# The down product of a feed-forward stage by seven block products, with y collected in the output

## What is computed

```
hm = rmsnorm(x, g_mlp_norm)
y  = x + square(relu(hm @ w_up)) @ w_down      # w_up 2048 x 8192, w_down 8192 x 2048, float32
```

## Time and profile before

| what | value |
|---|---|
| median of 3 runs | 2805.25 us (2804.82 to 2809.1) |
| profiled execution, its own time | 2809.45 us |
| its span, first to last instruction | 2808.0 us |
| mean granted TensorE clock | 0.996 of full speed |
| PE busy, share of the span | 99% |
| DVE / ACT / POOL busy | 56% / 34% / 8% |
| feed-forward stage | from 1412.9 us to the end |

### The profile page before, as it was taken

The page is one execution under the profiler, slowest core; times in us unless marked ns, Lnnn a source line. Parts: engine busy times, 40 slices in busy tenths (PEclk is TensorE's granted clock), DMA queues, the critical chain, the costliest instruction groups (busy, mean ns, idle before and its releaser), DMA issues.

```text
span 2808.0 us, 57688 instructions
## 1 busy us (share of the span) xinstructions
PE 2790.3 (99%) x22723; PEld 2745.9 (98%) x22723; DVE 1578.6 (56%) x2763; ACT 960.5 (34%) x1484; POOL 224.3 (8%) x341
## 2 busy tenths in 40 slices
PE   8999999999999999999999999999999999999999
PEld 8999999999999999999999999999999999999999
DVE  6433544454444454445576556665556665566658
ACT  5435433333333342222243223332233332333322
POOL 2100122210000010013300000000000000000000
PEclk9999999999999999999999999999999999999999
DMA  6533233322222224444433333332333323333235
GB/s 199 185 100 106 81 111 97 109 95 92 96 87 94 88 90 151 136 126 137 135 110 99 97 97 113 104 104 90 101 115 105 99 81 103 97 105 97 91 96 186
DMA packets 89562, 309.39 MB, mean 110 GB/s; under 512 B 11714, under 2 KB 12098, under 8 KB 89360
## 3 DMA queue, kind: packets, MB, share of 16 engines
q1 hardware_dynamic: 70112, 247.49, 27.8%
q0 software_dynamic: 16208, 55.42, 6.1%
q10 hardware_dynamic: 3168, 5.45, 0.6%
HBM read 287.23 MB, written 27.37 MB: 112 GB/s over the span
## 4 chain that ended last, share of the span: by engine, by line
PE 75%; issue 18%; DVE 3%; POOL 2%; ACT 1%; DMA 1%; POOLq 0%; SPq 0%; ACTq 0%; DVEq 0%
PE mm L540 25%; PE aux L919 13%; PE mm L919 13%; PE mm L863 12%; PE aux L863 9%; PE mm L614 1%; PE aux L645 1%; POOL z L2090 1%; DVE w_lo L1769 1%; ACT w_hi L1197 0%; PE aux L761 0%; POOL merge_d L2091 0%; DVE w_lo L1287 0%; PE aux L554 0%; PE aux L659 0%
## 5 line engine op out<-in xcount | busy, mean ns | idle before, releaser
L1287 DVE TENSOR_TENSOR w_lo<-w_raw,w_hi 128x512 fp32r<-128x512 f32 x392 | 283.3, 724 | 630.5 <-ACT w_hi L968 629.5
L1769 DVE TENSOR_TENSOR w_lo<-w_raw,w_hi 128x1024 fp32r<-128x1024 f32 x288 | 352.9, 1225 | 390.8 <-ACT w_hi L1197 158.1
L540 PE MATMUL mm<-a_hi,w_hi 128*128 128x260 f32 x2624 | 550.1, 291 | 3.2 <-DVE rel_s L1322 1.6
L540 PE MATMUL mm<-a_hi,w_lo 128*128 128x260 f32 x2624 | 532.1, 285 | 0.0
L540 PE MATMUL mm<-a_lo,w_hi 128*128 128x260 f32 x2624 | 532.1, 285 | 0.0
L1197 ACT ACTIVATE w_hi<-w_raw 128x1024 fp32r<-128x1024 f32 x288 | 297.5, 1057 | 661.0 <-PE mm L919 431.2
L968 ACT ACTIVATE w_hi<-w_raw 128x512 fp32r<-128x512 f32 x392 | 246.4, 629 | 692.8 <-PE mm L540 672.6
L540 PEld LDWEIGHTS mm<-a_hi,w_hi 128*128 128x128 f32 x2624 | 409.0, 191 | 10.2 <-DVE w_lo L1287 3.0
L540 PEld LDWEIGHTS mm<-a_lo,w_hi 128*128 128x128 f32 x2624 | 409.5, 191 | 0.0
L540 PEld LDWEIGHTS mm<-a_hi,w_lo 128*128 128x128 f32 x2624 | 408.3, 190 | 0.0
L863 PE MATMUL mm<-at_t,w_hi 128*128 128x260 f32 x2048 | 373.3, 284 | 1.1 <-DVE w_lo L1769 1.1
(11 more groups left out here) (320 smaller groups left out, 4161.4 us busy)
## 6 DMA issues: line engine op xcount, KB each, us to landing
w_raw<-in_w_ff SPq DMA_DIRECT2D x256, 512.0 KB, 3.6
w_raw<-in_w SPq DMA_DIRECT2D x200, 512.0 KB, 3.6
merge_d<-z POOLq DMA_DIRECT2D x32, 260.0 KB, 2.4
g_in<-merge_d POOLq DMA_DIRECT2D x16, 520.0 KB, 4.9
x_back<-x_d POOLq DMA_DIRECT2D x8, 520.0 KB, 9.1
pages<-in_cache_cmp POOLq DMA_DIRECT2D x16, 256.0 KB, 3.3
w_cmp<-in_w_cmp POOLq DMA_DIRECT2D x8, 512.0 KB, 4.8
stage<-in_cache_sel POOLq DMA_DIRECT2D x32, 128.0 KB, 2.5
```

Of the source, the lines that this page charges most:

```text
L540: last = pe.matmul(mm[:, 2 * v + h, 0:HT], w, a[:, kt, h * HT:(h + 1) * HT], start=first and k == 0 and part == 0, stop=final and k == CK ...
L1287: dve.tensor_tensor(w_lo[:, c, :], raw(u, c), w_hi[:, c, :].bitcast(F32), ALU.subtract).then_inc(lo_split, 1)
L1769: dve.tensor_tensor(ring_lo(i), fold(source(i)), ring_hi(i).bitcast(F32), ALU.subtract).then_inc(ff_lo, 1)
```

## The change

- The down part also goes by seven block products. A group's 16 y tiles are taken in four pieces (D0 to D3) of four y tiles; a piece is two row pairs (m = 0, 1), and each has seven products of 2 contraction steps times 3 matmuls. The contraction of 512 rows is one block row pair of 2 x 256.
- The hidden tiles become the token side of that product. They need the same seven combinations (B11 ... T2): three sums per r, made by POOL (`hidden_sums`), and their hi and lo (`hidden_hi`, `hidden_lo`) over all seven, in the arrays `fb_mid` and `fb_end`. The norm's factor is now multiplied in at the hidden rows (`hidden`, with `r_ff`), and ACT takes the square.
- Each piece needs weight sums: one (a21 + a22) by POOL (`weight_sum`), two by DVE (`down_sum`). The same sum of the up pairs moves from DVE to POOL. A piece has four hi and lo entries, three of 128x1024 and one of 128x512.
- The results of a piece are copied from PSUM by ACT (`copies`, `copy_c21`), combined by DVE (`cs_in`) in `y_mid`, and added to `y_t` in DRAM by two DMAs of 520 KB with `accum_op` on POOL's queue (`tiles_added`). `y_acc` and the ending `y_out` are gone; x2, the residual, is stored to `y_t` itself.
- The order is turned: the down pieces of group g-1 stand between the up parts of group g: U0, D0, D1, U1, D2, D3. Group 0 has U0 and U1 alone, and a last round has D0 to D3 alone. lo too has a ring of three buffers.

The core of the diff:

```diff
+            def up_part(p):                                   # PE
+                for b in range(2):
+                    pe.wait_ge(ff_lo, p.e + b + 1)
...
+                    product(p, b)
+                up_rest(p)
...
+            def down_product(p, b, m, js=(0, 1)):
+                hi, lo = ring_hi(p.slot(D_ENTRY[b])), ring_lo(p.slot(D_ENTRY[b]))
+                dst = bank((2 if b == 1 else 4 if b in (3, 5) else p.x) + m)
+                fb = fb_of(p.g - 1)
+                for j in js:
+                    o = m * 2 * P + j * P
+                    wh, wl = (w[:, D_SIDE[b], o:o + P] for w in (hi, lo))
+                    o = TIMES[b] * HT
+                    for w, e, part in ((wh, o, 0), (wh, A_HALF + o, 1), (wl, o, 2)):
+                        last = pe.matmul(dst, w, fb[:, j, e:e + HT],
...
-            def down_part(g, u, kts, hs=(0, 1)):
...
-                    for w, a, part in ((wh, fb_hi, 0), (wh, fb_lo, 1), (wl, fb_hi, 2)):
-                        for h in hs:
-                            last = pe.matmul(bank(o + h), w, a[:, kt, h * HT:(h + 1) * HT],
...
+            def freed_by_down(p, k):                          # SP
+                sp_.wait_ge(ff_lo, p.e + 3 + k)
+                return p.slots[k]
...
+            def up_part(p):                                   # DVE
...
+                    ff_lo_in(p, 1)
+                    up_sum(p, 1)
...
+                    if conv:
+                        hidden_lo(p.g - 1, 0, 0)
+                    ff_lo_in(p, 2)
+                ff_lo_in(p, 3)
+                if conv:
+                    hidden_lo(p.g - 1, 0, 1)
+                up_sum(p, 2)
+                ff_lo_in(p, 4)
...
+            def down_part(p):
...
+                    ff_lo_in(p, 1)
+                    down_sum(p, 1)
+                ff_lo_in(p, 2)
+                if not late:
+                    cs_in(p, 0)
+                ff_lo_in(p, 3)
...
+                if to and to.up:
+                    ff_lo_in(to, 0)
+                    up_sum(to, 0)
+                if whole(p.g, NG - 1) and p.n == D3:
+                    for n in range(2):
+                        hidden_lo(NG - 1, 0, n)
+                cs_in(p, 1)
+                cs_in(p, 2)
...
+            def weight_sum(p):                                # POOL
+                if p.up:
+                    a21, a22 = (w_raw[:, n, :] for n in p.slots[2:])
+                    pool.wait_ge(ff_sum, p.sums + 1)
+                    pool.wait_ge(ff_loaded[p.slots[3]], p.loads())
+                else:
+                    a21, a22 = (w_raw[:, p.slots[0], k * CW:(k + 1) * CW] for k in range(2))
+                    pool.wait_ge(ff_loaded[p.slots[0]], p.loads())
+                pool.tensor_tensor(a21, a21, a22, ALU.add).then_inc(ff_s1, 1)
+
+            def hidden_sums(g, r):
...
+                pool.tensor_tensor(ts[:, 0:2, :], c[:, 1:4:2, :], c[:, 0:2, :], ALU.subtract).then_inc(t_made, 1)
+                pool.wait_ge(t_made, n + 1)
+                pool.tensor_tensor(ts[:, 2, :], c[:, 3, :], ts[:, 0, :], ALU.subtract).then_inc(t_made, 1)
+                pool.wait_ge(t_made, n + 2)
+                pool.tensor_tensor(c[:, 1, :], c[:, 2, :], ts[:, 2, :], ALU.subtract).then_inc(t_made, 1)
+
+            def tiles_added(p):
+                y, first = y_buffer(p)
+                pool.wait_ge(ff_read, p.read + 3)
+                pool.wait_ge(ff_c21, p.c21 + 2)
...
+                for m in range(2):
+                    k = 4 * p.q + 2 * m
+                    pool.dma_start(t["y_t"][k:k + 2].rearrange("m p (h c) -> p m h c", h=2), y[:, m, :, :, :],
+                                   accum_op=ALU.add).then_inc(y_added[first + m], 16)
...
+            def body(g):
+                weight_sum(Part(g, U0))
+                if not whole(g, 1):
+                    tiles_added(Part(g - 1, D3))
+                window(g)
+                hidden_sums(g - 1, 1)
+                weight_sum(Part(g, D0))
+                weight_sum(Part(g, D1))
+                tiles_added(Part(g, D0))
+                weight_sum(Part(g, U1))
+                tiles_added(Part(g, D1))
+                hidden_sums(g, 0)
+                weight_sum(Part(g, D2))
+                weight_sum(Part(g, D3))
+                tiles_added(Part(g, D2))
```

More of the change, by code:

```diff
@@ L511, in _ @@
+            loads(1)
+            with sp_.Fori(2, NG - 1) as g:
+                loads(g)
+            loads(NG - 1)
+            for m in (D0, D1):
+                for k in range(2):
+                    n = freed_by_down(Part(NG, m), k)
+                    load_downs(NG, 2 + TILE_OF[m], n, SLOTS_LAST[D2 if m == D0 else D3])
         @block.tensor
@@ L944, in _ @@
[L944 to L953 removed]
+                product(p, 0, [KP - 1])
+                product(p, 1, [KP - 2, KP - 1])
+                up_rest(p)
+            def down_product(p, b, m, js=(0, 1)):
[8 more added lines that the diff above has]
+                        last = pe.matmul(dst, w, fb[:, j, e:e + HT],
+                                         start=FRESH[b] and j == 0 and part == 0, stop=j == 1 and part == 2,
+                                         skip_group_check=not FRESH[b])
+                if 1 in js:
+                    last.then_inc(ff_used, 1)
@@ L956, in _ @@
+            body(1)
+            with pe.Fori(2, NG - 1) as g:
+                body(g)
+            body(NG - 1)
+            down_parts(NG, (D0, D1, D2, D3))
         @block.scalar
@@ new lines, in copies, with copy_c21 @@
+            def copies(p, n):
+                dst, first = y_buffer(p)
+                for m in range(2):
+                    act.wait_ge(ff_used, p.used + (1, 5, 7, 9)[n] + m)
+                    if n == 0 and not whole(y_uses(p), 0):
+                        act.wait_ge(y_added[first + m], 16 * y_uses(p))
+                    run(dst[:, m, (0, 0, 1, 1)[n], (0, 1, 1, 0)[n], :], bank((4 if n == 2 else p.x) + m), ACT.Copy
+                        ).then_inc(ff_copied, 1)
+            def copy_c21(p, m=0):
+                act.wait_ge(ff_used, p.used + (NP if p.up else 2 * NP - 1 + m))
+                act.wait_ge(ff_read, p.read + 2)
+                dst = hid[p.pair][:, 2, :] if p.up else y_buffer(p)[0][:, m, 1, 0, :]
+                run(dst, bank(p.x + m), ACT.Copy).then_inc(ff_c21, 1)
@@ new lines, in _ @@
+            for n in UPS:
+                weight_sum(Part(0, n))
+            hidden_sums(0, 0)
+            body(1)
+            with pool.Fori(2, NG - 1) as g:
+                body(g)
+            body(NG - 1)
+            hidden_sums(NG - 1, 1)
+            weight_sum(Part(NG, D0))
+            tiles_added(Part(NG - 1, D3))
+            window(NG)
+            weight_sum(Part(NG, D1))
+            tiles_added(Part(NG, D0))
+            weight_sum(Part(NG, D2))
+            tiles_added(Part(NG, D1))
@@ L2153 @@
+            weight_sum(Part(NG, D3))
+            for n in (D2, D3):
+                tiles_added(Part(NG, n))
+            for n in range(4):
+                pool.wait_ge(y_added[n], 32 * NG - 16)
+                pool.wait_ge(y_added[4 + n], 16)
+            pool.wait_ge(win_stored, 16 * NG)
 _INS = ["x_t", "w", "w_ff", "gains", "one_hot", "rel_bias", "w_00", "table", "w_cmp", "pos", "cache_cmp", "cache_sel",
```

818 lines of the change are left out of this document (477 added, 341 removed).

## The result

The changed kernel takes 2796.23 us at the median of seven runs (2792.85 to 2799.04), the kernel before 2806.55 us beside it. The ratio is 0.9964 [0.9952, 0.9975], so it is faster by 0.36%: the sign is the forecast one, but the time lies 45 us above 2751 and outside the range of 2722 to 2790.

The account below looks back on a forecast made before the run. PE, busy for 99% of the span, was taken to bound the kernel. Fewer matmuls (-92.4 us), stalls (+27) and ends (+11) summed to -54.4, from 2805.25 to 2751 us; range 2722 to 2790.

Parts of the forecast that it names:

- the adds do not bound the stage: Against a 7% rival: eight adding DMAs a group bound the stage, 2952 us at 12 us an add.
- 1.8 us a group, 27 us in 15 groups (bounds 0 and 37): Up parts: POOL's sums hold DVE through their lock, so PE waits for product 2; 1.8 us a group, 27 us.
- last group: D3 of group 15 holds four hidden_lo on DVE, 12.8 us against PE's 10.1: +2.5 us.
- 768 matmuls: Down part: 48 fewer matmuls a group in 16 groups, at 0.1203 us each: 92.4 us less.
- stalls of the stage: Groups' up parts: PE waits because POOL's sums delay DVE's chain: +27 us, bounds 0 and 37.
- start and first conversion: POOL's first weight_sum over DVE's last token operands, +2 us; first down round's hidden work ahead of a hi, +2 us.
- tail: After the last matmuls: copy, cells, two issues and a 520 KB landing, 6.4 to 10.1 us against 4.0: +4.5 us.
- walk of the first chain: U0, product 1 to 2: POOL's weight_sum delays DVE's lo; product 2 comes 1.5 us late, hidden_sums included.
- price of POOL's sums: POOL: 2.02 ns a column, 2.1 us for a sum of 1024 columns, 1.05 for 512; 12.7 us a group.
- late load: Rival, 17%: U0's product 1 weights land late beside the adding DMAs, 6.5 us of landing; 39 us more, 2790 us.
- first conversion: First down round: hidden(0, 1) and its squares stand ahead of hi of product 2 in group 1: +2 us.
- does not become the bound: DVE, each group: its 62 us plus POOL's 12.7 make 75 us, which fit in PE's 80.8.

Follow-up runs that it names:

- e_plain: The changed kernel with plain stores of y, which overwrite and do not add: 2787.9 us, ratio 0.9934.
- s_adds: The changed kernel with its adding DMAs carrying 16 of the 128 partitions, same number of DMAs: 2808.0 us, ratio 1.0003.
- s_all: The changed kernel with all of POOL's sums in the stage cut to one column, except the first and last hidden_sums: 2755.9 us, ratio 0.9820.
- s_all_ring: s_all with the weight buffer slots dealt out anew, so that product 1's block comes into the slot freed first: 2739.5 us, ratio 0.9764.
- s_load: The changed kernel with the last weight block each up part waits for carrying 16 of 128 partitions: 2789.5 us, ratio 0.9942.
- v_weight: The changed kernel with the six weight sums of a group made by DVE instead of POOL: 2836.2 us, ratio 1.0106.
- v_all: The changed kernel with all sums, weight_sum and hidden_sums, on DVE; POOL only issues DMAs: 2824.1 us, ratio 1.0060.
- n_up: The changed kernel with only the up weight sum on DVE, before product 2's lo, and hidden_lo behind that lo: 2848.7 us, ratio 1.0145.

## Why the prediction missed

Right were the count (21,955), the rate (80.74 us a group without stalls), the DVE and PE mechanism, and that the adds do not bound the stage. Wrong were sizes, first of all **the step "1.8 us a group, 27 us in 15 groups (bounds 0 and 37)"**: it is 3.15 us a group by the rate, 47 us. Next comes the last group, put at 2.5 us and 18 us in fact. On the profiled spans (2808.0 to 2793.9, -14.1 us, forecast -54.4):

| term | forecast | measured | from |
|---|---|---|---|
| 768 matmuls | -92.4 | -92.4 | count and rate |
| stalls of the stage | +27 | +45 | PE's gaps, 46.4 against 1.5 |
| start and first conversion | +4 | +10 | PE's gaps, 13.3 against 2.9 |
| last group | +2.5 | +18 | PE's gaps in the last round, 18.2 against -0.1 |
| tail | +4.5 | +7 | 11.2 against 4.1 |
| before the stage | 0 | -2 | its first matmul at 1410.7 against 1413.0 |

The gaps are my sum over the timeline of PE of the time between starts beyond 0.1203 us a matmul: the start is the first 504 matmuls of the stage, the last round the last 336. The right column adds to -14, the span's own difference. The code before the stage is the same, and in the profiles of the other kernels the stage starts between 1407 and 1415 us, so the last line is no effect of the change. In the start and the last round 73 matmuls start at the 0.50 clock; they are 7 us of those gaps.

- **The stalls of the stage**, some 20 us short, 8 to 10 us above my upper bound. The walk of the first chain was close: after U0's start on PE (1799.11) the lo of product 1 ends at 2.69 us, where I had 2.7, and the lo of product 2 at 6.19, where I had 6.3. Wrong is what follows. I let POOL begin hidden_sums at about 5.05 and put 1.5 us on product 2 of U0; they begin at 8.57 (1807.68, behind an idle time of 1.80 us that DVE's second hidden_lo ends), and product 2 is 0.5 late. I put 0.9 on product 2 of U1; it is 0.7. What the walk missed are product 6 of U0 (1.0), where I wrote that the other products had over 1 us of cover, and product 1 of U1 (0.6). It followed one chain in one part; the lock's delays travel on through ACT's in-order queue (hidden_hi with hi behind it) to later products. The four places sum to 2.8 us in the group shown, of 3.15 by the rate.
- **The price of POOL's sums** was near: 2.1 us for 1024 columns, from a row whose two inputs are the same tile. The trace has 2.70 us, but each of the 32 sums of that size starts during a DVE operation with both inputs in SBUF, and from DVE's end on it takes 2.24 to 2.28 us; and 512 columns take 1.26 when nothing disturbs them (2725.13 above). What I left out is that wait, 0.4 us in the group shown. The Trainium skill (GPSIMD Engine Reference, section 3.1) gives 4497 ns for 2048 columns, an estimate of 2.25 us for 1024: the trace agrees with it, once the wait is taken off.
- **The late load** was a rival at 17%, in U0 and 39 us large, because of the adding DMAs. It exists, but in U1 alone. There the block is asked for when D1's last lo ends (1836.9) and takes 5.5 us to land; at the median of the groups it is 5.3 us in U1 and 3.5 in U0. I had allowed 5.2. Two y stores are issued beside it (at 1837.31), but the add is not the reason: with plain stores (e_plain) it is 6.1 us, with an eighth of the data (s_adds) 4.8. It is worth 16 us when nothing else is late (s_all to s_all_ring) and 7 us in the kernel as it is (s_load).
- **The last group**: I counted the four hidden_lo (+2.5) and not that POOL's queue stands 15.67 us for D2's copies with the next round's sums behind it. The order of POOL's queue stands in the diff; I never walked it there.
- **The first conversion**, +2 by me, is a pause of 3.2 us at 1469.90: POOL's hidden_sums and weight sum lie end to end from 1460.4 to 1467.6 over DVE's sum and `hidden`. Another of 2.5 us, at 1453.47, I had no term for: a lo stands on DVE behind an operation of the norm (L2115), which waits 5.54 us for ACT.
- **The tail**: two adding issues take 2.41 us and not 1.2; from the second one's end to the end of the span 7.4 us pass.
- **DVE "does not become the bound"** holds for its throughput (834 us busy of 1000) and fails as a statement on the schedule: v_weight, v_all and n_up moved some 2.4 to 8 us of sums a group onto it (two of 1024 columns in n_up, all of them in v_all) and lost 28 to 52 us, some of it by the clock (of n_up's 52 us, 15).

That POOL's sums cost 40 us and the late load 16 us is shown by taking each away. The traces show the lock in each place, but how much of the 40 us is the lock and how much the length of the sums in the chain is not shown. That the kernel would reach 2740 us with all its work done is not shown: no version that does all sums has a median below 2793. A longer ring or a second `t_sum` buffer, which would give the chain cover, was not tried.

## What to carry to other kernels

When a change puts work on an engine that shares a lock with the one feeding TensorE, walk every product of a whole period, with each in-order queue that a delay can travel through, and do the same for the first and the last period; busy shares (65% and 29% here) told nothing. Take the price of an operation from a row with the same operands, not only the same size, and take off what it waited for the other engine. Where the cover is under one instruction of the other engine, any edit, even one that takes work away (s_adds), can cost more than the work is worth, and a stall that grows longer can cost PE's clock besides, so read the granted clock before you put a difference down to stalls. Test an edit by leaving the work out first, which bounds what a better order can give.

## What the runs showed that I had not expected

- Less work made it slower: adding DMAs of an eighth of the data gave 12 us more. POOL arrives earlier and one stall of a group grows from 0.7 to 2.1 us; the stalls of 1000 us grow by 4 us in all, the matmuls at the 0.50 clock behind the long ones by 12.
- POOL's weight sum of 1024 columns lasts 2.70 us in the mean, but it takes 2.24 to 2.28 from the moment that DVE's operation ends. A length in a trace holds the wait for the lock, on either engine.
- An adding DMA costs its issuer two thirds more than a plain one, 2.41 us for two against 1.45, and 520 KB land in 7.8 us against 4.7 at the median, two thirds longer. Into SBUF 512 KB took 9.2 us. The Trainium skill (Collectives: The Full Stack, "The bandwidth ceiling: the fold count and why AG ≠ RS ≠ AR") puts the add of a reducing collective at a second read, half the rate of a copy; the landing times, two thirds longer, agree roughly.
- POOL's small sums of 260 columns take 0.74 us undisturbed and 1.61 beside DVE (means 1617 and 1612 ns in the stage). DVE's operations of that stretch start between them (1808.65, 1811.25), so a chain of short sums is stretched most.
- Around the pause of 8.69 us the granted clock falls to 0.50 and is 1.00 again from 2738.2; its mean is 0.83 in 2720 to 2760, and in the 29 us of that window beside its two pauses (8.85 and 2.06 us) the 203 matmuls start 0.14 us apart instead of 0.12: a long stall costs more than its length.
